# Index scores and attention logits in three rounded products instead of two-pass float32, with the splits on ScalarE and VectorE

## The chip, the cores and the metric

The program runs on one core of a Trainium2 chip. Its engines work side by side and meet through semaphores: PE (TensorE, the matrix products), ACT (ScalarE), DVE (VectorE), POOL (GpSimd) and SP (SyncE, which issues the DMAs). The metric is the device time of one execution in microseconds (us), as the median over runs.

## The reference, cut to what matters

Two layers, each with a feed-forward block, a token mixer, a second feed-forward block and an embedding block, on 256 tokens of 1024 features in float32. The change lies in the token mixer, in the two products below:

```
sc = jnp.einsum('bqhd,bsd->bqhs', qib, ki32)                 # index scores: 8 heads of 64, one key for all heads
I = jnp.einsum('bqh,bqhs->bqs', wib * idx_scale, relu(sc))   # summed over heads; the top 64 keys of a query are kept
...
logits = jnp.einsum('bqhd,bqkhd->bqhk', qb, ksel) * att_scale  # attention logits: 8 heads of 64
prob = softmax(logits masked to the kept keys); out = prob @ v
```

Queries are taken in two blocks of 128. A query of the first block can only see the first 128 keys, one of the second all 256.

## The kernel before, in words

**Weights.** All large products run as chunks: 2048 columns of weights per partition come by DMA into one of three slots of `raw`; ACT rounds them to `w_hi` (float32r, line 903), DVE subtracts to get the rest `w_lo` (line 1303), and PE multiplies in three rounded terms, hi by hi, lo by hi, hi by lo (lines 408 to 410). Such a rounding and rest together are called a split, `split(L, n)`, and stand in the code of ACT and of DVE at fixed places. PE waits for the rest of a slot before it starts the chunk. The chunks of the mixer are numbered from MIX: IQ is MIX+3 and +4 (index queries), GQ +5, GK +6, AQ +7 and +8 (attention queries), AK +9 and +10 (attention keys), GV +11 and +12, GR +13 and +14, and MGA from +15.

**Order.** Nothing is scheduled by a tool: each engine runs its instructions in the order of its function, and PE's order is one long row of chunks with small products between them. Results pass through 8 banks of PSUM; `drained` counts, for each bank, the copies out of it, and `wait_drained` and `wait_free` wait on that count.

**Index scores.** ACT copies the two chunks of index queries from PSUM to `iqT` (line 999). DVE scales the index key into `ikT` (line 1449), and a small DMA (line 361, semaphore `keys_copied`) copies it to the other half of the partitions. After chunk IQ+1 PE runs two transposes (line 571) and then `scores` four times (line 542), each for two heads by two: the heads r = 0 and r = 1 sit in the lower and the upper 64 partitions and write different banks. The operands are plain float32. The trace shows each such matmul as two records of PE and two of its weight loads.

**Attention logits.** ACT copies the queries to `qT` (lines 1028, 1031), DVE scales the keys into `kT` (lines 1498, 1505). `logits(j)` (line 603) multiplies 64 queries at a time, in tiles of 64 by 64 of the array, so four products stand side by side. PE calls `logits(0)` between chunk GV+1 and chunk GR, after four transposes (line 619), once the banks of `aq1` and `ak1` are drained; `logits(2)`, `(4)` and `(6)` come in the loop over MGA, each right behind `levels` (line 690, also 64 by 64). `scores(0)` and `(2)`, `logits(0)` and `(2)` work on 128 keys, the other four calls on 256.

**DVE in this part.** After the scores DVE adds up the heads, picks the top 64 keys of the first query block (`top_k(L, 0)`), makes the decays, picks those of the second block (`top_k(L, 1)`, with `ak0` taken halfway), takes `ak1` and then does splits MIX+13 to MIX+16 in a row. It then waits for the logits.

Of the kernel before, what the change touches and what calls it, by code (L numbers as in the profile page):

```python
# [7 lines left out]
F32 = mybir.dt.float32  # L8
F32R = mybir.dt.float32r
# [4 lines left out]
P = 128  # L14
# [78 lines left out]
def hybrid_trunk(nc, a, out):  # L93
    L_N = a["gla_gate_w2"].shape[0]
    with ExitStack() as ctx:
# [6 lines left out]
        def sem(name):  # L102
            return ctx.enter_context(nc.semaphore(name))
# [37 lines left out]
        pT_hi_, pT_lo_ = (b[:, 2, :].rearrange("p (k t) -> p k t", t=T) for b in (small_hi, small_lo))  # L141
        zg = silu
# [32 lines left out]
        qT = sb("qT", [P, 4, T])  # L175
# [3 lines left out]
        kT = sb("kT", [P, 4, T])  # L179
# [47 lines left out]
        keys_copied = sem("keys_copied")  # L227
        p_landed = sem("p_landed")
# [170 lines left out]
        def _(pe):  # L399
# [123 lines left out]
            def mix(L):  # L523
# [9 lines left out]
                def scores(qT_, kT_, name, j):  # L533

                    qt, _, m = STEPS[j]
                    nk = P * (qt + 1)
                    for r in range(2):
                        wait_free(pe, L, f"{name}{j + r}")
                    for i in range(2):
                        for r in range(2):  # L540
                            rows = slice(64 * r, 64 * r + 64)
                            mm = pe.matmul(bank[BANK_OF[f"{name}{j + r}"]][:, i * nk:(i + 1) * nk], qT_[rows, 2 * m + i, qt * P:(qt + 1) * P],  # L542
                                           kT_(rows, 2 * m + i, nk), start=True, stop=True)
                            if i:
                                done(mm, f"{name}{j + r}")
# [27 lines left out]
                pe.wait_ge(keys_copied, (L + 1) * 16)  # L573
                for j in range(0, 8, 2):
                    if j < 4:
                        wait_drained(pe, L, f"iq{j // 2}")
                    scores(iqT, lambda rows, hp, nk: ikT[rows, 0 if rows.start else 1, 0:nk], "sc", j)
# [14 lines left out]
                def logits(j):  # L592

                    qt, _, m = STEPS[j]
                    nk = P * (qt + 1)
                    for r in range(2):
                        wait_free(pe, L, f"lg{j + r}")
                    for i in range(2):
                        for r in range(2):
                            rows = slice(64 * r, 64 * r + 64)  # L600
                            for c in range(2):
                                at = qt * P + 64 * c
                                mm = pe.matmul(bank[BANK_OF[f"lg{j + r}"]][64 * c:64 * c + 64, i * nk:(i + 1) * nk],  # L603
                                               qT[rows, 2 * m + i, at:at + 64], kT[rows, 2 * m + i, 0:nk], start=True, stop=True)
                            if i:
                                done(mm, f"lg{j + r}")
# [282 lines left out]
        def _(act):  # L889
# [99 lines left out]
            def mix(L):  # L989
# [6 lines left out]
                split(L, MIX + 5)  # L996
                for i in range(2):
# [30 lines left out]
                take(L, "aq0", flat(qT[:, 0:2, :]))  # L1028
                split(L, MIX + 10)
                chunk_products(L, AQ + 1)  # L1030
                take(L, "aq1", flat(qT[:, 2:4, :]))
# [9 lines left out]
                split(L, MIX + 14)  # L1041
                chunk_products(L, GV + 1)
# [247 lines left out]
        def _(dve):  # L1290
# [148 lines left out]
            def mix(L):  # L1439
# [10 lines left out]
                split(L, MIX + 5)  # L1450
                split(L, MIX + 6)
                split(L, MIX + 7)
# [42 lines left out]
                def take_first_keys():  # L1495

                    chunk_products(L, AK)
                    take(L, "ak0", kT[:, 0:2, :])
# [6 lines left out]
                take(L, "ak1", kT[:, 2:4, :])  # L1505
                split(L, MIX + 13)
                split(L, MIX + 14)
                split(L, MIX + 15)
# [369 lines left out]
```

## Time and profile before

| | |
|---|---|
| median of 3 runs | 1175.69 us (1175.69 to 1175.87) |
| profiled execution: its own time | 1175.69 us |
| profiled execution: span from first to last instruction | 1173.9 us |
| mean granted clock of TensorE | 0.998 of full speed |
| PE busy | 1166.0 us, 99% of the span |
| PE weight loads busy | 1142.5 us, 97% |
| DVE, ACT, POOL busy | 820.7, 610.0, 117.3 us |

The time of a run is the span and some 1.8 us around it. A PE share of 99% says that hardly any moment of the span has no matmul record. PE's records overlap (one lasts longer than the step to the next), so the cost of a matmul is read from the distance of starts, not from its own length.

### The profile page before, as it was taken

What the parts mean: (1) busy time and instruction counts of PE and PEld (TensorE: products, weight loads), DVE (VectorE), ACT (ScalarE), POOL (GpSimd) and SP (SyncE); (2) the same over time, 40 slices, a digit from 0 to 9 for tenths busy, and PEclk for the clock granted to TensorE, in tenths of its full rate; (3) what the DMA queues carried; (4) which work ended last, traced back from release to release, by engine and by line L of the source; (5) the groups of instructions that cost most, each with busy time, mean ns of one, the idle gap of its engine ahead of it and who ended that gap; (6) DMA issues with size and microseconds to landing.
All of it is one profiled execution on the core that took longest, in us unless ns stands there. A gap on an engine that the chain in (4) does not pass through costs nothing.

```text
span 1173.9 us, 24028 instructions
## 1 busy us (share of the span) xinstructions
PE 1166.0 (99%) x10518; PEld 1142.5 (97%) x10518; DVE 820.7 (70%) x936; ACT 610.0 (52%) x689; POOL 117.3 (10%) x130
## 2 busy tenths in 40 slices
PE   9999999999999999999999999999999999999998
PEld 9999999999999999999999999999899999999997
DVE  6866545697978766655786665458799787666556
ACT  6544445555745644444764443447466555444455
POOL 2000001011512000001110000100134020000011
PEclk9999999999999999999999999999999999999999
DMA  8655555545445555555546555554644456655551
GB/s 296 230 203 189 190 204 176 188 150 204 152 145 194 202 193 201 191 188 196 192 179 220 184 205 186 184 213 141 218 146 149 140 207 210 203 184 201 190 180 37
DMA packets 33528, 218.87 MB, mean 186 GB/s; under 512 B 5200, under 2 KB 6544, under 8 KB 7440
## 3 DMA queue, kind: packets, MB, share of 16 engines
q1 hardware_dynamic: 33424, 217.34, 53.5%
q8 instruction: 83, 1.36, 0.5%
q14 instruction: 21, 0.17, 0.0%
HBM read 216.15 MB, written 1.05 MB: 185 GB/s over the span
## 4 chain that ended last, share of the span: by engine, by line
PE 98%; DMA 1%; DVE 0%; ACT 0%; SPq 0%; DVEq 0%; issue 0%
PE psum L408 32%; PE psum L409 31%; PE psum L410 31%; PE psum L690 1%; PE psum L669 1%; DMA x_all<-in_x 1%; PE psum L542 0%; PE psum L603 0%; PE psum L653 0%; PE psum L724 0%; DVE gates L1795 0%; PE psum L638 0%; PE psum L735 0%; PE psum L758 0%; DVE hB_lo L1763 0%; PE psum L585 0%
## 5 line engine op out<-in xcount | busy, mean ns | idle before, releaser
L1303 DVE TENSOR_TENSOR w_lo<-raw,w_hi 128x2048 fp32r<-128x2048 f32 x200 | 457.9, 2293 | 218.7 <-ACT w_hi L903 218.5
L903 ACT ACTIVATE w_hi<-raw 128x2048 fp32r<-128x2048 f32 x201 | 385.2, 1916 | 352.2 <-PE psum L410 344.3
L408 PE MATMUL psum<-hA_hi,w_hi 128*128 128x256 f32 x1360 | 377.6, 278 | 0.0
L409 PE MATMUL psum<-hA_hi,w_lo 128*128 128x256 f32 x1360 | 375.7, 276 | 0.0
L410 PE MATMUL psum<-hA_lo,w_hi 128*128 128x256 f32 x1360 | 375.6, 276 | 0.0
L408 PEld LDWEIGHTS psum<-hA_hi,w_hi 128*128 128x128 f32 x1360 | 255.3, 188 | 2.7 <-issue 2.7
L409 PEld LDWEIGHTS psum<-hA_hi,w_lo 128*128 128x128 f32 x1360 | 255.3, 188 | 0.0
L410 PEld LDWEIGHTS psum<-hA_lo,w_hi 128*128 128x128 f32 x1360 | 255.3, 188 | 0.0
L408 PE MATMUL psum<-hB_hi,w_hi 128*128 128x256 f32 x832 | 229.9, 276 | 1.0 <-DVE w_lo L1771 1.0
L409 PE MATMUL psum<-hB_hi,w_lo 128*128 128x256 f32 x832 | 229.7, 276 | 0.0
L410 PE MATMUL psum<-hB_lo,w_hi 128*128 128x256 f32 x832 | 229.7, 276 | 0.0
L410 PE MATMUL psum<-hid_lo,w_hi 128*128 128x256 f32 x704 | 194.3, 276 | 0.0
L408 PE MATMUL psum<-hid_hi,w_hi 128*128 128x256 f32 x704 | 194.3, 276 | 0.0
L409 PE MATMUL psum<-hid_hi,w_lo 128*128 128x256 f32 x704 | 194.3, 276 | 0.0
L408 PEld LDWEIGHTS psum<-hB_hi,w_hi 128*128 128x128 f32 x832 | 156.2, 188 | 1.4 <-DVE w_lo L1771 1.4
L409 PEld LDWEIGHTS psum<-hB_hi,w_lo 128*128 128x128 f32 x832 | 156.2, 188 | 0.0
L410 PEld LDWEIGHTS psum<-hB_lo,w_hi 128*128 128x128 f32 x832 | 156.2, 188 | 0.0
L410 PEld LDWEIGHTS psum<-hid_lo,w_hi 128*128 128x128 f32 x704 | 132.1, 188 | 0.0
L409 PEld LDWEIGHTS psum<-hid_hi,w_lo 128*128 128x128 f32 x704 | 132.1, 188 | 0.0
L408 PEld LDWEIGHTS psum<-hid_hi,w_hi 128*128 128x128 f32 x704 | 132.1, 188 | 0.0
L1223 POOL TENSOR_TENSOR total<-silu 128x256 f32<-128x256 f32 x9 | 9.9, 1102 | 612.9 <-ACT silu L913 612.9
L1382 DVE TENSOR_TENSOR gates<-psum,rb 128x512 f32<-128x512 f32 x44 | 30.3, 690 | 38.7 <-PE psum L410 38.7
(208 smaller groups left out, 1240.7 us busy)
## 6 DMA issues: line engine op xcount, KB each, us to landing
raw<-in_weights SPq DMA_DIRECT2D x203, 1024.0 KB, 4.9
raw<-in_weights SPq DMA_DIRECT2D x2, 512.0 KB, 6.2
out<-gates SPq DMA_DIRECT2D x4, 192.0 KB, 2.2
x_all<-in_x SPq DMA_DIRECT2D x1, 520.0 KB, 3.9
x_all<-in_x SPq DMA_DIRECT2D x1, 512.0 KB, 6.3
relu<-in_p SPq DMA_DIRECT2D x2, 256.0 KB, 5.0
consts<-in_consts SPq DMA_DIRECT2D x1, 384.0 KB, 5.6
out<-gates SPq DMA_DIRECT2D x2, 128.0 KB, 2.0
```

The source lines that it names most:

```text
L408: pe.matmul(o, lh, rh, start=start, stop=False)
L409: pe.matmul(o, ll, rh, start=False, stop=False)
L410: return pe.matmul(o, lh, rl, start=False, stop=stop)
L669: mm = pe.matmul(bank[BANK_OF[f"oa{n}"]][64 * r:64 * r + 64, i * P:(i + 1) * P], v[:, kt, h * 64:(h + 1) * 64], probT[r][:, q * P:(q + 1) ...
L690: mm = pe.matmul(bank[BANK_OF[f"lv{p}{hh}"]][64 * c:64 * c + 64, first + q * cols:first + (q + 1) * cols], kk[rows, q * P + 64 * c:q * P + ...
L903: act.activation(w_hi[:, s, :], raw[:, s, :], ACT.Copy).then_inc(hi_ready[s], 1)
L1223: pool.tensor_tensor(total[:, :], squared[:, 0, :], squared[:, 1, :], ALU.add).then_inc(sq_added, 1)
L1303: dve.tensor_tensor(w_lo[:, s, :], raw[:, s, :], w_hi[:, s, :].bitcast(F32), ALU.subtract).then_inc(lo_ready[s], 1)
L1382: dve.tensor_tensor(up_sum, products(2 * g + 1), both(rb), ALU.mult).then_inc(up_scaled, 1)
```

## The change: three rounded terms, and who makes them

Both products are now made like the weight chunks: operands are split into a rounded part and a rest, and each product is the sum of three float32r matmuls. The logits take 128 queries at a time. The queries are split while they leave PSUM: ACT writes the rounded part, DVE subtracts it from PSUM, and it is DVE's instruction that now frees the bank. The index key is split after its DMA (two copies on ACT, two subtractions on DVE). The attention keys are scaled by DVE as before, into the place of `iqT`, then rounded by ACT and subtracted by DVE. The other parts of the program are as they were. The diff, cut to its core:

```diff
+        iq_hi, iq_lo = oa_hi, oa_lo
+        q_hi, q_lo = obT_hi, obT_lo
+        ik_hi, ik_lo = (b[:, :, :].rearrange("p a t -> p (a t)") for b in (diag_hi, diag_lo))
...
-        qT = sb("qT", [P, 4, T])
+        k_hi = sb("k_hi", [P, 4, T], F32R)
-        kT = sb("kT", [P, 4, T])
+        k_lo = sb("k_lo", [P, 4, T], F32R)
...
PE, scores:
-                    for i in range(2):
-                        for r in range(2):
-                            rows = slice(64 * r, 64 * r + 64)
-                            mm = pe.matmul(bank[...][:, i * nk:(i + 1) * nk], qT_[rows, 2 * m + i, qt * P:(qt + 1) * P],
-                                           kT_(rows, 2 * m + i, nk), start=True, stop=True)
+                        for term, (q, key) in enumerate(((iq_hi, ik_hi), (iq_lo, ik_hi), (iq_hi, ik_lo))):
+                            for r in range(2):
+                                rows = slice(64 * r, 64 * r + 64)
+                                mm = pe.matmul(bank[...][:, i * nk:(i + 1) * nk], q[rows, 2 * m + i, qt * P:(qt + 1) * P],
+                                               key[rows, 0:nk], start=term == 0, stop=term == 2)
-                pe.wait_ge(keys_copied, (L + 1) * 16)
+                pe.wait_ge(ik_lo_ready, (L + 1) * 2)
PE, logits:
-                            for c in range(2):
-                                at = qt * P + 64 * c
-                                mm = pe.matmul(bank[...][64 * c:64 * c + 64, i * nk:(i + 1) * nk],
-                                               qT[rows, 2 * m + i, at:at + 64], kT[rows, 2 * m + i, 0:nk], start=True, stop=True)
+                        for term, (q, key) in enumerate(((q_hi, k_hi), (q_lo, k_hi), (q_hi, k_lo))):
+                            for r in range(2):
+                                mm = pe.matmul(bank[...][:, i * nk:(i + 1) * nk], q[rows, 2 * m + i, qt * P:(qt + 1) * P],
+                                               key[rows, 2 * m + i, 0:nk], start=term == 0, stop=term == 2)
PE, before logits(0):
-                        for name in ("aq1", "ak1"):
-                            wait_drained(pe, L, name)
+                        wait_drained(pe, L, "aq1")
+                        pe.wait_ge(k_lo_ready, (L + 1) * 2)
ACT:
-                    take(L, f"iq{i}", flat(iqT[:, 2 * i:2 * i + 2, :]))
+                    act.activation(flat(iq_hi[:, 2 * i:2 * i + 2, :]), bank[BANK_OF[f"iq{i}"]][:, :], ACT.Copy).then_inc(iq_hi_ready, 1)
                     if i == 0:
                         split(L, MIX + 6)
+                        act.wait_ge(keys_copied, (L + 1) * 16)
+                        for rows, at in copied:
+                            act.activation(ik_hi[rows, :], ikT[rows, at, :], ACT.Copy).then_inc(ik_hi_ready, 1)
...
                 split(L, MIX + 14)
+                for i in range(2):
+                    wait_drained(act, L, f"ak{i}")
+                    act.activation(k_hi[:, 2 * i:2 * i + 2, :], iqT[:, 2 * i:2 * i + 2, :], ACT.Copy).then_inc(k_hi_ready, 1)
                 chunk_products(L, GV + 1)
DVE (rest_of_bank waits for the rounded part, subtracts it from the bank, and counts the bank as drained):
                 split(L, MIX + 6)
+                rest_of_bank(iq_hi_ready, iq_hi, iq_lo, "iq0", 0)
+                for i, (rows, at) in enumerate(((slice(0, 64), 1), (slice(64, 128), 0))):
+                    dve.wait_ge(ik_hi_ready, L * 2 + i + 1)
+                    dve.tensor_tensor(ik_lo[rows, :], ikT[rows, at, :], ik_hi[rows, :].bitcast(F32), ALU.subtract).then_inc(ik_lo_ready, 1)
+                rest_of_bank(iq_hi_ready, iq_hi, iq_lo, "iq1", 1)
                 split(L, MIX + 7)
...
                 distance(64, 63)
+                rest_of_bank(q_hi_ready, q_hi, q_lo, "aq0", 0)
                 split(L, MIX + 11)
+                rest_of_bank(q_hi_ready, q_hi, q_lo, "aq1", 1)
                 top_k(L, 1, halfway=take_first_keys)
...
                 split(L, MIX + 13)
                 split(L, MIX + 14)
+                for i in range(2):
+                    dve.wait_ge(k_hi_ready, L * 2 + i + 1)
+                    dve.tensor_tensor(k_lo[:, 2 * i:2 * i + 2, :], iqT[:, 2 * i:2 * i + 2, :], k_hi[...].bitcast(F32),
+                                      ALU.subtract).then_inc(k_lo_ready, 1)
                 split(L, MIX + 15)
                 split(L, MIX + 16)
```

On PE, the first call of the logits, between the transposes of line 619 (now 628) and chunk GR, stood so:

```order
L619 MATMUL psum<-consts,klev 128x128 x4
L603 MATMUL psum<-kT,qT 64x128 x8
```

and stands now so (`small_hi` and `small_lo` hold the split queries):

```order
L628 MATMUL psum<-consts,klev 128x128 x4
L612 MATMUL psum<-k_hi,small_hi 128x128 x2
L612 MATMUL psum<-k_hi,small_lo 128x128 x2
L612 MATMUL psum<-k_lo,small_hi 128x128 x2
L612 MATMUL psum<-k_hi,small_hi 128x128 x2
L612 MATMUL psum<-k_hi,small_lo 128x128 x2
L612 MATMUL psum<-k_lo,small_hi 128x128 x2
```

Eight products of 64 queries became twelve of 128, with a rest of the keys among their operands.

On DVE, from the second half of `top_k(L, 1)` to the first logits, the order was:

```order
L1437 TENSOR_SCALAR selbias<-score 128x256
L1420 TENSOR_TENSOR kT<-psum,rb 128x512
L1303 TENSOR_TENSOR w_lo<-raw,w_hi 128x2048 x4
L1521 TENSOR_TENSOR relu<-psum,selbias 128x256
```

and is now:

```order
L1453 TENSOR_SCALAR selbias<-score 128x256
L1436 TENSOR_TENSOR iqT<-psum,rb 128x512
L1319 TENSOR_TENSOR w_lo<-raw,w_hi 128x2048 x2
L1540 TENSOR_TENSOR k_lo<-iqT,k_hi 128x512 x2
L1319 TENSOR_TENSOR w_lo<-raw,w_hi 128x2048 x2
L1555 TENSOR_TENSOR relu<-psum,selbias 128x256
```

The subtractions that finish the attention keys stand behind the splits of MIX+13 and MIX+14. Ahead of `top_k(L, 1)` there are two more subtractions:

```order
L1521 TENSOR_TENSOR dist<-bcum 128x512
L1471 TENSOR_TENSOR small_lo<-psum,small_hi 128x512
L1319 TENSOR_TENSOR w_lo<-raw,w_hi 128x2048
L1471 TENSOR_TENSOR small_lo<-psum,small_hi 128x512
L1445 MEMSET score 64x64
```

where before the `dist` instruction, one `w_lo` and the MEMSET followed each other.

On DVE ahead of the scores, the three splits of MIX+5 to MIX+7 that stood in a row now have the rests of the index queries and of the key between the second and the third:

```order
L1319 TENSOR_TENSOR w_lo<-raw,w_hi 128x2048 x2
L1471 TENSOR_TENSOR small_lo<-psum,small_hi 128x512
L1478 TENSOR_TENSOR diag_lo<-ikT,diag_hi 64x256 x2
L1471 TENSOR_TENSOR small_lo<-psum,small_hi 128x512
L1319 TENSOR_TENSOR w_lo<-raw,w_hi 128x2048
L1491 TENSOR_SCALAR score<-relu,wi 128x128
```

## Rows read from the trace of the kernel before

**Rows 1.** The page: chain of work that ended last, by engine.

```profile
PE 98%; DMA 1%; DVE 0%; ACT 0%; SPq 0%; DVEq 0%; issue 0%
```

**Rows 2.** Waits of PE, the longest: us in total, times, longest.

```profile
PE psum L855 <- POOL ones_r L1235: 1.2, 1, 1.2
```

**Rows 3.** Chain of work in time: start us, us; a 256-key call.

```profile
295.11 0.89 PE psum L603 x16
```

**Rows 4.** Timeline, PE weight loads: start us, us, line, shape.

```profile
214.43 2.58 PEld L542 LDWEIGHTS psum<-ikT,iqT 64*128 64x128 f32 x32 [0.17 <-issue]
...
217.34 0.19 PEld L408 LDWEIGHTS psum<-hA_hi,w_hi 128*128 128x128 f32 x1 [0.33 <-issue]
217.45 0.19 PEld L409 LDWEIGHTS psum<-hA_hi,w_lo 128*128 128x128 f32 x1
...
262.62 0.42 PEld L603 LDWEIGHTS psum<-kT,qT 64*64 64x64 f32 x16 [0.17 <-issue]
263.22 0.19 PEld L408 LDWEIGHTS psum<-w_hi,hA_hi 128*128 128x128 f32 x1 [0.17 <-issue]
```

**Rows 5.** The same view: calls 2 and 4 of the logits, levels to attend.

```profile
281.63 0.43 PEld L603 LDWEIGHTS psum<-kT,qT 64*64 64x64 f32 x16
282.23 0.20 PEld L653 LDWEIGHTS psum<-consts,prob 128*128 128x128 f32 x2 [0.17 <-issue]
...
294.43 0.56 PEld L690 LDWEIGHTS psum<-amat,silu 64*64 64x64 f32 x32
294.90 0.65 PEld L603 LDWEIGHTS psum<-kT,qT 64*64 64x64 f32 x16
295.93 0.13 PEld L669 LDWEIGHTS psum<-probT,v 128*64 128x64 f32 x1 [0.39 <-issue]
...
323.57 0.33 PEld L690 LDWEIGHTS psum<-amat,silu 64*64 64x64 f32 x16
323.94 0.13 PEld L669 LDWEIGHTS psum<-probT,v 128*64 128x64 f32 x1
```

**Rows 6.** Weight loads of 128 columns by form: end sums of one column, transposes.

```profile
1165.82 0.41 PEld L871 LDWEIGHTS psum<-ones_r,total 128*128 128x128 f32 x3
...
L653 PEld LDWEIGHTS psum<-consts,prob 128*128 128x128 f32 x48 | 5.4, 139 | 0.3 <-issue 0.3
```

**Rows 7.** Timeline, ACT and DVE, ahead of the scores.

```profile
214.32 0.60 ACT L984 ACTIVATE iqT<-psum 128x512 f32<-128x512 f32 x1 [3.04 <-PE psum L410]
...
211.32 2.29 DVE L1303 TENSOR_TENSOR w_lo<-raw,w_hi 128x2048 fp32r<-128x2048 f32 x1 [3.13 <-ACT w_hi L903]
216.82 2.29 DVE L1303 TENSOR_TENSOR w_lo<-raw,w_hi 128x2048 fp32r<-128x2048 f32 x1 [3.22 <-ACT w_hi L903]
```

**Rows 8.** Timeline, DVE, from the last keys on.

```profile
259.20 0.68 DVE L1420 TENSOR_TENSOR kT<-psum,rb 128x512 f32<-128x512 f32 x1
259.80 4.48 DVE L1303 TENSOR_TENSOR w_lo<-raw,w_hi 128x2048 fp32r<-128x2048 f32 x2
265.39 2.29 DVE L1303 TENSOR_TENSOR w_lo<-raw,w_hi 128x2048 fp32r<-128x2048 f32 x1 [1.11 <-ACT w_hi L903]
```

**Rows 9.** The same place in layer 1: PE loads and DVE.

```profile
840.67 0.43 PEld L603 LDWEIGHTS psum<-kT,qT 64*64 64x64 f32 x16 [0.17 <-issue]
...
837.80 4.48 DVE L1303 TENSOR_TENSOR w_lo<-raw,w_hi 128x2048 fp32r<-128x2048 f32 x2
```

**Rows 10.** Durations (ns min/median/max) of a subtraction or product in SBUF.

```profile
L1385 DVE TENSOR_TENSOR gates<-gates x44: 691/692/694, 30.4 to 1078.7; 128x512 f32<-128x512 f32 x44
L1356 DVE TENSOR_TENSOR diag_lo<-total,diag_hi x6: 410/418/420, 24.6 to 1144.1; 128x256 fp32r<-128x256 f32 x6
```

**Rows 11.** Clock: warm-up matmuls; windows at the end (busy, PEclk third from last).

```profile
1.21 6.03 PE L855 MATMUL psum<-ones_r 128*128 128x128 f32 x36 [1.21 <-POOL ones_r L1235]
...
1166.40:1168.80 2.40, 1.83 (x12) 1.40 (x11) 1.62 (x8) 1.89 (x6) 0.00 (x0) 1.00 0.00 0
1168.80:1170.00 1.20, 0.00 (x0) 0.00 (x0) 1.20 (x4) 0.00 (x0) 0.00 (x0) 0.53 0.18 63
```

More of the change, by code:

```diff
@@ L227, in hybrid_trunk @@
         keys_copied = sem("keys_copied")
+        ik_hi_ready = sem("ik_hi_ready")
+        ik_lo_ready = sem("ik_lo_ready")
+        iq_hi_ready = sem("iq_hi_ready")
+        q_hi_ready = sem("q_hi_ready")
+        k_hi_ready = sem("k_hi_ready")
+        k_lo_ready = sem("k_lo_ready")
         p_landed = sem("p_landed")
@@ L531, in chunk, with scores @@
                     return s
-                def scores(qT_, kT_, name, j):
+                def scores(j):
                     qt, _, m = STEPS[j]
@@ L537, in scores @@
                     for r in range(2):
-                        wait_free(pe, L, f"{name}{j + r}")
+                        wait_free(pe, L, f"sc{j + r}")
                     for i in range(2):
-                        for r in range(2):
-                            rows = slice(64 * r, 64 * r + 64)
-                            mm = pe.matmul(bank[BANK_OF[f"{name}{j + r}"]][:, i * nk:(i + 1) * nk], qT_[rows, 2 * m + i, qt * P:(qt + 1) * P],
-                                           kT_(rows, 2 * m + i, nk), start=True, stop=True)
-                            if i:
-                                done(mm, f"{name}{j + r}")
+                        for term, (q, key) in enumerate(((iq_hi, ik_hi), (iq_lo, ik_hi), (iq_hi, ik_lo))):
+                            for r in range(2):
+                                rows = slice(64 * r, 64 * r + 64)
+                                mm = pe.matmul(bank[BANK_OF[f"sc{j + r}"]][:, i * nk:(i + 1) * nk], q[rows, 2 * m + i, qt * P:(qt + 1) * P],
+                                               key[rows, 0:nk], start=term == 0, stop=term == 2)
+                                if i and term == 2:
+                                    done(mm, f"sc{j + r}")
                 for t in range(2):
@@ L576, in mix @@
                         wait_drained(pe, L, f"iq{j // 2}")
-                    scores(iqT, lambda rows, hp, nk: ikT[rows, 0 if rows.start else 1, 0:nk], "sc", j)
+                    scores(j)
                 chunk(GQ, "gq")
@@ L598, in logits @@
                     for i in range(2):
-                        for r in range(2):
-                            rows = slice(64 * r, 64 * r + 64)
-                            for c in range(2):
-                                at = qt * P + 64 * c
-                                mm = pe.matmul(bank[BANK_OF[f"lg{j + r}"]][64 * c:64 * c + 64, i * nk:(i + 1) * nk],
-                                               qT[rows, 2 * m + i, at:at + 64], kT[rows, 2 * m + i, 0:nk], start=True, stop=True)
-                            if i:
-                                done(mm, f"lg{j + r}")
+                        for term, (q, key) in enumerate(((q_hi, k_hi), (q_lo, k_hi), (q_hi, k_lo))):
+                            for r in range(2):
+                                rows = slice(64 * r, 64 * r + 64)
+                                mm = pe.matmul(bank[BANK_OF[f"lg{j + r}"]][:, i * nk:(i + 1) * nk], q[rows, 2 * m + i, qt * P:(qt + 1) * P],
+                                               key[rows, 2 * m + i, 0:nk], start=term == 0, stop=term == 2)
+                                if i and term == 2:
+                                    done(mm, f"lg{j + r}")
                 for n, c in [(GV, "gv"), (GR, "gr")]:
@@ L1027, in mix @@
                 chunk_products(L, AQ)
-                take(L, "aq0", flat(qT[:, 0:2, :]))
+                act.activation(flat(q_hi[:, 0:2, :]), bank[BANK_OF["aq0"]][:, :], ACT.Copy).then_inc(q_hi_ready, 1)
                 split(L, MIX + 10)
                 chunk_products(L, AQ + 1)
-                take(L, "aq1", flat(qT[:, 2:4, :]))
+                act.activation(flat(q_hi[:, 2:4, :]), bank[BANK_OF["aq1"]][:, :], ACT.Copy).then_inc(q_hi_ready, 1)
                 split(L, MIX + 11)
```

10 lines of the change are left out of this document (8 added, 2 removed).

## The prediction

> **What bounds the kernel now.** I read the page first: the chain of work that ended last is PE for 98% of the span [rows 1]. The view of waits is the second: PE waits at three places, all at the start or the end of the span, and the longest wait is 1.2 us [rows 2]. So between these PE runs without a break. Each microsecond that the change adds to PE's row of loads and matmuls, or in which PE finds an operand unfinished, is a microsecond of the whole, since PE has no later wait in which it could be made up. The other engines count only where they make PE wait. So there are three questions: what the new products cost PE, when the split operands are ready, and when PE would want them. The third view is the timeline of PE's weight loads, whose starts are exact; the fourth is the timeline of ACT and DVE at the same places. Times below are those of layer 0.
>
> **PE: the unit prices.** A plain float32 matmul is two passes. With 256 keys a call of the logits takes 0.89 us for four steps (two values of i, two passes; the tiles beside each other share a step), 0.22 us a step [rows 3]. With 128 keys the whole call takes, from its first load to the next chunk's, 0.60 us [rows 4], and a step is some 0.11 us. A rounded term is one pass: the loads of chunks with 256 columns are 0.11 us apart [rows 4]. A rounded term with only 128 columns is nowhere in the trace. Upper bound: the same 0.11 to 0.12. Lower bound: the transposes, whose two loads are 0.20 - 0.14 = 0.06 us apart [rows 5, 6]. I take 0.11, since the load itself sets it: at the end three loads of 128 columns, each with a matmul of one column, take 0.41 us, that is (0.41 - 0.19) / 2 = 0.11 us a step though almost nothing is streamed [rows 6], and the loads of rounded chunks last 0.19 us like these, not 0.14 us like the transposes' [rows 4, 6]. So three terms cost 0.34 us. That is 0.10 us less than two passes with 256 keys (0.44) and 0.12 us more than two passes with 128 (0.22). There are as many steps of one kind as of the other, so in bare products the change gives PE next to nothing.
>
> On this the Trainium skill, TensorE: Matmul & The Clock Gate, section Back-to-back issue gap, gives about 56 ns for a warm matmul of 128 columns counted by itself. By it the 24 terms a layer with 128 columns would be 0.055 us cheaper each, 1.3 us a layer. Its section on LDWEIGHTS gives 107 ns for a load of 128 columns, and with that the row at the end of the trace agrees.
>
> **PE: the scores.** The key's rest must be ready. DVE ends split MIX+6 at 211.32 + 2.29 = 213.61 [rows 7]. Behind it come the rest of iq0 (0.69 us as other work on 512 elements [rows 10]; the next instruction starts 0.08 before its end) to 214.2, and two rests of the key at 0.42 [rows 10] less the same overlap, to 214.83. ACT has rounded the key by 211.9 (two short copies behind its split, whose end at 211.3 is what DVE's split waits for [rows 7]), so DVE is last. With 0.05 us for the semaphore PE starts at 214.90 instead of 214.43 [rows 4]: a wait of 0.47. The first call takes 6 steps, 0.67 us, to 215.57. The second needs the rest of iq1: ACT ends its rounding at 214.92 [rows 7], DVE's subtraction follows to 215.66, so the call starts at 215.72. Then 17 steps of 0.114 to the last load at 217.66. The way out: behind a 256-key call of the logits the next load is 295.93 - (294.90 + 0.65 - 0.13) = 0.51 us after the last load of the call, behind a 128-key call 263.22 - (262.62 + 0.42 - 0.13) = 0.31 us [rows 4, 5], in both cases two of the call's last steps and 0.09. A rounded 256-column term has a step of 0.11, so 0.31. Chunk GQ then loads at 217.98 instead of 217.34 [rows 4]: **+0.64 us**.
>
> **DVE: how late the attention keys are.** From 219 us on DVE has no idle time until the pair of splits ends at 264.3; I read the timeline row by row, and its end stands in [rows 8]. The subtractions inserted ahead of the scores end at 215.7, in the 3.22 us in which DVE waited for ACT [rows 7], so they cost DVE nothing. The two rests of the attention queries are different: they stand where DVE is full, and add 2 times 0.61 = 1.22 us to all that follows. The take of ak1 moves from 259.20 to 260.42 and the pair of splits from 259.80 to 261.02 [rows 8]. The next instruction can start 4.40 us later, so the rests of the keys start at 265.42. ACT has rounded the keys long before: ak1 is drained at 261.1, plus some 0.6. Two subtractions of 128x512 in SBUF, 0.61 and 0.69 us [rows 10], end at **266.71**.
>
> **PE: the first logits.** PE would load for them at 262.62 + 0.64 = 263.26 [rows 4]. Before, it only needed the take of ak1, done at 259.88 [rows 8]. Now it needs the rests, at 266.71 + 0.05. **The wait is 3.50 us.** Behind PE's waiting load stands all the rest of the layer. No weight chunk adds to it: MIX+13, the first half of the pair, ends at 262.1 + 1.22 = 263.3 and is wanted at 263.22 + 0.64 = 263.86 even without the wait [rows 4, 8], and behind the pair DVE had 1.11 us of idle time [rows 8]. The call itself: 5 steps of 0.112 and a way out of 0.27 (between 0.20 and 0.31) are 0.83 against 0.60 us: **+0.23**.
>
> **PE: the other calls.** Before, the logits' loads followed those of `levels` at once (294.90 against a last load at 294.43 + 0.56 - 0.13 = 294.86), since both use 64 by 64 tiles [rows 5]. Now the tile is 64 by 128. From `levels` to the attend products, another change of form, the step is 323.94 - (323.57 + 0.33 - 0.13) = 0.17 us [rows 5]. Call 2: 0.17 + 0.56 + 0.27 = 1.00 against 0.04 + 0.60 = 0.64 us (281.63 to 282.23) [rows 5]: **+0.36**. Calls 4 and 6: 0.17 + 0.57 + 0.31 = 1.05 against 1.07 us (294.86 to 295.93) [rows 5]: **0**.
>
> **The sum.** 0.64 + 3.50 + 0.23 + 0.36 = 4.73 us a layer. Layer 1 has the same distances: PE's load for the first logits starts 2.87 us behind DVE's pair of splits, in layer 0 it is 2.82 us [rows 4, 8, 9]. Twice 4.73 is 9.5 us. The profiled execution's own time is 1175.69 us and so is the median, so I predict **1185.2 us**, 0.8% slower.
>
> **The rivals.**
>
> *The clock falls in the wait.* At the end of the trace PE has 12 matmul records in 2.40 us, still at a granted clock of 1.00; in the next 1.2 us, with none, the mean is 0.53 [rows 11], so it went from 2.4 to 1.2 GHz behind a thin stretch. In the forecast PE does nothing for 3.50 us, twice. The price of coming back is bounded by the warm-up: 36 loads in 6.03 us [rows 11], where 36 steps of 0.11 would be 4.0, so 2.0 us. With one fall 1187.2, with two 1189.2. Against it: in the chunks before and behind the wait PE is dense, which it was not at the end of the trace. The same page of the Trainium skill, section HAM oscillation, says that a PE which idles between bursts of matmuls is put back to half clock and pays for it each time; by that rule both layers pay. I give 22% to one or both.
>
> *The two heads do not run beside each other when rounded.* The plain float32 tiles of 64 rows do. The trace has no rounded matmul on 64 rows. If each pair cost two steps, the 24 pairs of the scores and the 24 of the logits a layer are 2.7 us each. But PE would then want the keys 2.7 us later and wait 0.8 instead of 3.5: 0.64 + 2.7 + 0.8 + 0.23 + 0.36 + 2.7 = 7.4 us a layer, 1190.6. 7%, since loads of both kinds have the same duration.
>
> *The keys are in time, the other side.* If DVE ended the rests of the keys when PE wants them, 3.5 us earlier than in my count, 1.23 us a layer stay: 1178.2. If the 128-column terms also ran at the 0.06 us of the transposes, 24 of them would save 1.2 us a layer and the time would be 1175.7, no slower than before. It decides at 263.2 us, the end of `k_lo`. For it speaks only that the order of DVE could be shortened by something that I count as full; against it, the pair of splits alone ends at 264.3 before anything is added [rows 8]. 8%, of which 3 for slower. (The cheap terms alone, with the wait, give about 1184: PE comes earlier and waits longer, so only what lies behind the wait is gained.)
>
> *The forecast*: 63%, 1183.5 to 1186.5.
>
> **How the numbers follow.** A measurement of this kernel tells about 0.2% (2.4 us) from no change. Faster by more takes the last rival and something yet unseen, 2%; within 0.2% 3%; the rest is slower, 95%. For the range I leave out the keys in time and the serial heads, and reach from the forecast with its cheap bounds (128-column terms at 0.06, the wait some tenths shorter: 1183.0) to the clock falling in both layers (1189.2).
>
> **What the profile after would show.** PE's waits should have a new row at the logits' line for DVE's `k_lo`, two times 3.5 us, and one at the scores' line for DVE's rests, about 0.5 us a layer. DVE's busy time grows by some 9 us. The loads of the rounded terms on 64 rows should come in pairs, 0.11 us from pair to pair for 128 and for 256 keys. The granted clock stays near 0.998; a fall right behind the wait is the first rival. The prediction is wrong if `k_lo` does not end 3.5 us, give or take 0.5, behind PE's arrival, or if the pairs are 0.06 or 0.22 us apart.

## The result and the profile after

The changed kernel takes **1190.84 us** (median of 4 runs, 1190.43 to 1191.04), the kernel before 1175.70 beside it: a ratio of 1.0128, 95% interval 1.0115 to 1.0140, 15.1 us slower. The forecast was 1185.2 with a range to 1189.2, so the sign is right, the size is too small by 5.6 us, and the time lies outside the range.

The view of cores of the changed kernel (span, mean granted clock of TensorE; before it was 1173.9 us and 0.998), then its page, parts 1 and 4:

```profile
core 0: 1189.2 us, clock 0.993
```

```profile
PE 1173.0 (99%) x10518; PEld 1150.4 (97%) x10518; DVE 829.4 (70%) x952; ACT 614.1 (52%) x697; POOL 117.2 (10%) x130
...
PE 97%; DVE 1%; issue 1%; DMA 1%; ACT 0%; SPq 0%; DVEq 0%
```

The chain is still PE [rows 1], but it has two gaps ("issue", 1%). PE's waits, to compare with [rows 2] (us in total, times, longest):

```profile
PE psum L612 <- issue: 7.6, 2, 3.8
PE psum L864 <- POOL ones_r L1251: 1.2, 1, 1.2
PE psum L552 <- DVE diag_lo L1478: 1.1, 2, 0.5
```

L612 is the logits' product, L552 the scores'. The view names "issue" for the wait of 3.8 us, not DVE; the timelines show whom it is for. DVE and PE's loads around the first logits call of layer 0, for [rows 8] and [rows 4] (the first two rows of DVE are from further ahead; the part on the prediction comes back to them):

```profile
217.06 2.29 DVE L1319 TENSOR_TENSOR w_lo<-raw,w_hi 128x2048 fp32r<-128x2048 f32 x1 [1.26 <-ACT w_hi L912]
...
232.63 0.30 DVE L1450 MAX8 top<-score 128x8 f32<-128x128 f32 x1 [0.52 <-DVE score L1452]
...
260.96 0.68 DVE L1436 TENSOR_TENSOR iqT<-psum,rb 128x512 f32<-128x512 f32 x1
261.56 4.48 DVE L1319 TENSOR_TENSOR w_lo<-raw,w_hi 128x2048 fp32r<-128x2048 f32 x2
265.96 1.28 DVE L1540 TENSOR_TENSOR k_lo<-iqT,k_hi 128x512 fp32r<-128x512 f32 x2
```

```profile
267.32 0.21 PEld L612 LDWEIGHTS psum<-k_hi,small_hi 64*128 64x128 f32 x2 [4.05 <-issue]
267.42 0.22 PEld L612 LDWEIGHTS psum<-k_hi,small_lo 64*128 64x128 f32 x2
...
267.87 0.22 PEld L612 LDWEIGHTS psum<-k_lo,small_hi 64*128 64x128 f32 x2
268.16 0.19 PEld L417 LDWEIGHTS psum<-w_hi,hA_hi 128*128 128x128 f32 x1
268.27 0.19 PEld L418 LDWEIGHTS psum<-w_hi,hA_lo 128*128 128x128 f32 x1
268.56 0.33 PEld L419 LDWEIGHTS psum<-w_lo,hA_hi 128*128 128x128 f32 x1
268.99 0.33 PEld L417 LDWEIGHTS psum<-w_hi,hA_hi 128*128 128x128 f32 x1
```

The rests of the keys end at 265.96 + 1.28 = 267.24, PE's first load starts at 267.32. The loads of the call come in pairs ("x2": both heads), 0.11 us from pair to pair. Then comes what the forecast did not have: from 268.56 on a load lasts 0.33 us instead of 0.19, and the loads are 0.43 us apart where the same loads of this chunk were 0.23 apart in the kernel before:

```profile
263.33 0.19 PEld L409 LDWEIGHTS psum<-w_hi,hA_lo 128*128 128x128 f32 x1
263.56 0.19 PEld L410 LDWEIGHTS psum<-w_lo,hA_hi 128*128 128x128 f32 x1
```

The windows (start and end, length, then the busy time of PE, its weight loads, DVE, ACT and POOL) show the granted clock, third from last, in the wait and behind it, and then behind the same wait in layer 1:

```profile
263.50:267.00 3.50, 0.01 (x1) 0.00 (x0) 3.50 (x4) 3.16 (x4) 0.00 (x0) 1.00 0.62 169
267.00:269.00 2.00, 1.65 (x15) 1.41 (x16) 2.00 (x2) 0.00 (x0) 0.00 (x0) 0.86 1.08 430
269.00:271.00 2.00, 2.00 (x6) 1.61 (x5) 0.45 (x1) 0.00 (x0) 0.00 (x0) 0.50 0.93 315
271.00:273.00 2.00, 2.00 (x8) 1.60 (x8) 0.00 (x0) 0.00 (x0) 0.00 (x0) 0.79 0.92 385
273.00:275.00 2.00, 2.00 (x10) 1.62 (x10) 0.00 (x0) 0.00 (x0) 0.00 (x0) 1.00 0.36 147
```

```profile
851.00:853.00 2.00, 0.84 (x8) 0.88 (x10) 2.00 (x3) 0.51 (x2) 0.00 (x0) 0.78 1.04 434
853.00:855.00 2.00, 2.00 (x11) 1.67 (x10) 1.26 (x1) 0.00 (x0) 0.00 (x0) 0.50 0.99 410
855.00:857.00 2.00, 2.00 (x6) 1.54 (x5) 0.00 (x0) 0.00 (x0) 0.00 (x0) 0.50 0.93 307
857.00:859.00 2.00, 2.00 (x6) 1.52 (x6) 0.00 (x0) 0.00 (x0) 0.00 (x0) 0.52 0.73 307
859.00:861.00 2.00, 2.00 (x10) 1.62 (x9) 0.00 (x0) 0.00 (x0) 0.00 (x0) 1.00 0.01 4
```

0.50 is 1.2 GHz of 2.4. In layer 0 the clock is still full in the wait itself, and PE had been at work again for over 1 us (from 267.32 to the load at 268.56) when it fell. The time lost is about the missing clock times the window: in layer 0 2 x (0.14 + 0.50 + 0.21) = 1.7 us, in layer 1 2 x (0.22 + 0.50 + 0.50 + 0.48) = 3.4 us.

**Where the 15.1 us are.** PE executes the same loads of weight chunks in the same order in both kernels. The start of each, less the start of the same load before, gives a shift; what it gains between two stations is the cost of what lies between. This table, worked out from the traces, holds those gains in us, layer 0 / layer 1, for the changed kernel and the experiments; everything not listed gains under 0.1 us, but for 0.47 us in e10, told there:

```
                        scores       first call   call 2       whole trace
                                     (to MGA0)
changed kernel          0.73 / 0.70  5.69 / 7.19  0.39 / 0.39  15.1
e1 late call            0.73 / 0.73  0.74 / 0.70  0.83 / 0.82   4.6
e2 rests between        0.70 / 0.70  1.94 / 1.90  0.39 / 0.39   6.0
e3 dummies in the wait  0.70 / 0.70  4.13 / 4.09  0.39 / 0.39  10.4
e4 logits only          0.01 / 0.01  7.51 / 5.91  0.39 / 0.39  14.2
e6 wait alone           0.00 / 0.00  6.66 / 5.81  0.00 / 0.00  12.5
e7 late, query early    0.63 / 0.63  0.84 / 0.75  0.82 / 0.85   4.5
e8 late, all orders     0.63 / 0.63  1.01 / 1.00  0.77 / 0.80   4.9
e9 before, late call    0.01 / 0.01 -0.35/ -0.35  0.98 / 1.01   1.3
e10 rests on GpSimd     0.69 / 0.71  1.17 / 3.47  0.39 / 0.39   7.4
```

For the changed kernel: scores 1.4, call 2 0.8, first calls 12.9. e3 has the same waits and, as told there, no fall of the clock: its first calls gain 4.13 and 4.09, which is 0.23 for the rounded call, as forecast, and 3.9 for the wait (the view of waits, which goes by matmuls, has 3.8). What the changed kernel has above that, 1.56 and 3.10, together 4.7 us, is the fall. It is a little less than the 5.1 us of missing clock, since at full clock these loads are 0.23 us apart and not half of 0.43.

### The profile page after: what moved, and what is told of

Same layout as the page of the kernel before. It is cut to its first block, busy times and chain, and to the rows that moved or that the text cites. A ratio compares the mean times of both kernels' runs of the same rounds, so it can differ in the third digit from the quotient of the medians.

```text
span 1189.2 us, 24052 instructions
## 1 busy us (share of the span) xinstructions
PE 1173.0 (99%) x10518; PEld 1150.4 (97%) x10518; DVE 829.4 (70%) x952; ACT 614.1 (52%) x697; POOL 117.2 (10%) x130
## 4 chain that ended last, share of the span: by engine, by line
PE 97%; DVE 1%; issue 1%; DMA 1%; ACT 0%; SPq 0%; DVEq 0%
PE psum L417 31%; PE psum L418 31%; PE psum L419 31%; PE psum L612 1%; PE psum L699 1%; PE psum L678 1%; DMA x_all<-in_x 1%; PE psum L552 1%; PE psum L662 0%; DVE w_lo L1319 0%; ACT w_hi L912 0%; PE psum L733 0%; DVE gates L1829 0%; PE psum L744 0%; PE psum L647 0%
## 5 line engine op out<-in xcount | busy, mean ns | idle before, releaser
L417 PE MATMUL psum<-hA_hi,w_hi 128*128 128x256 f32 x1360 | 377.6, 278 | 0.0
L417 PEld LDWEIGHTS psum<-hA_hi,w_hi 128*128 128x128 f32 x1360 | 255.4, 188 | 2.3 <-issue 2.0
L417 PE MATMUL psum<-hB_hi,w_hi 128*128 128x256 f32 x832 | 229.9, 276 | 0.7 <-DVE w_lo L1805 0.7
L417 PE MATMUL psum<-hid_hi,w_hi 128*128 128x256 f32 x704 | 194.3, 276 | 0.0
L417 PEld LDWEIGHTS psum<-hB_hi,w_hi 128*128 128x128 f32 x832 | 156.2, 188 | 1.1 <-DVE w_lo L1805 1.1
L417 PEld LDWEIGHTS psum<-hid_hi,w_hi 128*128 128x128 f32 x704 | 132.2, 188 | 0.0
```

Source lines behind the costliest of these rows:

```text
L417: pe.matmul(o, lh, rh, start=start, stop=False)
```

## The experiments

The experiments are numbered e1 to e10. Each time below is a median; the kernel before, run beside it on the same chip, took 1175.75 to 1175.83 us, and the ratio to it stands behind with its 95% interval. "Theory" is from e1 on: the wait costs its length, and the fall of the clock behind it some 5 us more.

**e1, the first logits call late** (behind the output-gate chunk GR):

```
                         done(mm, "kdT")
-                        wait_drained(pe, L, "aq1")
-                        pe.wait_ge(k_lo_ready, (L + 1) * 2)
-                        logits(0)
...
+                wait_drained(pe, L, "aq1")
+                pe.wait_ge(k_lo_ready, (L + 1) * 2)
+                logits(0)
                 wait_drained(pe, L, "kdT")
```

> The changed kernel, with the first call of the logits moved on PE from before chunk GR to behind it, some 11 us later; DVE and ACT keep their order. My theory (the wait for the rests of the keys and the clock that falls in it are 12.5 to 13 us of the 15.1, the products themselves the rest): the keys are ready long before PE wants them, no wait, clock near 0.998, and what stays is 0.72 us a layer at the scores, 0.38 at the second call and some 0.25 at the first, so 1178.4 us. Rival A (rounded products on 64 rows bring the clock down by themselves, wherever they stand): the clock stays near 0.993 and the time is near 1183. Rival B (the logits' mask on DVE and the exponentials behind it now come too late for the gates' chunks): a new PE wait behind MGA, more than 1180.

1180.29 us, 1.0038 [1.0023, 1.0053], clock 0.998. The wait and the fall are gone together, with 10.5 of the 15.1 us. It is 1.9 us above what was expected; its waits show two that were not there before, for a split of DVE (L417) and for the recurrent state (L662). Rival B, a new wait of PE and more than 1180, came in this form:

```profile
PE psum L552 <- DVE diag_lo L1478: 1.1, 2, 0.5
PE psum L417 <- DVE w_lo L1319: 0.9, 2, 0.5
PE psum L662 <- DVE state L1595: 0.8, 2, 0.4
```

**e2, the wait shorter**: the rests of the keys between the two splits, not behind them.

```
                 split(L, MIX + 13)
-                split(L, MIX + 14)
                 for i in range(2):
                     dve.wait_ge(k_hi_ready, L * 2 + i + 1)
                     dve.tensor_tensor(k_lo[:, 2 * i:2 * i + 2, :], iqT[:, 2 * i:2 * i + 2, :], k_hi[:, 2 * i:2 * i + 2, :].bitcast(F32),
                                       ALU.subtract).then_inc(k_lo_ready, 1)
+                split(L, MIX + 14)
```

> The changed kernel, with DVE's two subtractions for the keys moved ahead of split MIX+14 (behind MIX+13 as before), one split of 2.2 us earlier. My theory: PE's wait at the first logits falls from 3.8 to 1.6 us a layer, 4.4 us less in both; a wait of 1.6 us leaves the clock up, which gives 5.1 back: 1190.8 - 9.5 = 1181.3 us. If the clock falls even in the shorter wait: 1186.4. If the wait was not set by DVE's order but by ACT's roundings or the take of the keys, nothing moves: 1190.8.

1181.79 us (1181.65 to 1183.31), 1.0055 [1.0038, 1.0072].

```profile
PE psum L612 <- issue: 3.2, 2, 1.6
```

With 1.6 us of wait the clock stayed: window 267 to 269 us has 1.00. The fourth run, at 1183.31, is 1.5 us above the median with a mean clock of 0.997 where the other three have 0.998 and 0.999; e10 comes back to it.

**e3, the wait filled**: as the changed kernel, but PE works while it waits.

```
+                        wait_free(pe, L, "lg0")
+                        for _ in range(17):
+                            pe.matmul(bank[BANK_OF["lg0"]][:, 0:P], ones[:, :], ones[:, :], start=True, stop=True)
                         wait_drained(pe, L, "aq1")
```

> The changed kernel, with 17 matmuls of 128 by 128 that nobody reads (34 passes, some 3.8 us) in front of the wait for the keys, into the bank that the first logits overwrite. It leaves out nothing. PE is busy in the time in which it waited. My theory (the clock falls because PE does nothing there, and costs 5.1 us over both layers, 1.7 and 3.4): the wait stays as lost time, the clock stays up, 1185.7 us, give or take 0.5 for the length of the filling. Rival (the fall has another cause, as the rounded products): clock 0.993 again and 1190.8 us or more.

1186.07 us, 1.0088 [1.0072, 1.0103], clock 0.998. Timeline of PE (matmuls):

```profile
263.19 3.96 PE L632 MATMUL psum<-ones_r 128*128 128x128 f32 x34
267.20 0.33 PE L612 MATMUL psum<-k_hi,small_hi 64*128 64x128 f32 x2
```

From the last transpose before it to the first load of the call 4.19 us pass in layer 0, in both kernels, so the time for which nothing useful is done is the same, and still 4.8 us are gone: PE's idleness costs them, beyond its own length. The change plus products that nobody reads is faster than the change.

**e4, the logits only** (the scores, their queries and their key as before, none of the rests for them on DVE and ACT):

```
-                        for term, (q, key) in enumerate(((iq_hi, ik_hi), (iq_lo, ik_hi), (iq_hi, ik_lo))):
...
+                        for r in range(2):
+                            rows = slice(64 * r, 64 * r + 64)
+                            mm = pe.matmul(bank[BANK_OF[f"{name}{j + r}"]][:, i * nk:(i + 1) * nk], qT_[rows, 2 * m + i, qt * P:(qt + 1) * P],
+                                           kT_(rows, 2 * m + i, nk), start=True, stop=True)
...
-                rest_of_bank(iq_hi_ready, iq_hi, iq_lo, "iq0", 0)
```

> Only the logits in three rounded terms; the index scores stay in plain float32, the key's DMA is waited for by PE as before. My theory: PE arrives 0.72 us earlier a layer at the first logits while DVE is hardly earlier, so the wait grows to 4.3 us and the scores' cost turns into wait: 1175.7 + 2 x (4.3 + 0.25 + 0.38) + 5.1 for the clock = 1190.7 us, the same as the full change. Rival (the costs of the two parts add): 1190.8 - 1.4 = 1189.4 us.

1189.52 us, 1.0117 [1.0102, 1.0132], nearer the rival than the theory: the waits are 4.1 us at most, 0.3 longer than in the changed kernel, since DVE comes earlier too (its rests of the keys end at 266.86, not 267.24). The profiled execution is the slowest of its four, 1190.09. Here layer 0 has the long fall and layer 1 the short one (7.51 / 5.91 in the table; the changed kernel has 5.69 / 7.19).

**e5, the scores only** (the mirror of e4: the logits, their queries and keys as before).

> The index scores in three rounded terms, the attention logits in float32 as before. In the changed kernel the loads of the chunk behind the scores started 0.72 us (layer 0) and 0.71 us (layer 1) later, 0.5 us of it the wait for the key's rest. Theory (the two halves add up): 1175.8 + 1.4 = 1177.2 us, clock as before, no wait at the first logits call. Rival (the scores' later vector work is what costs at the logits too): the vector engine's 1.7 us of rests come back as a wait at the attention's own keys, 1178.5 us or more.

1177.16 us, 1.0011 [1.0002, 1.0021], as expected to 0.1 us. Its profiled execution took 6214.8 us, for a reason that nothing here shows, and no row of it is read; that PE does not wait at the first logits follows from the time alone. The two halves add up: e4's 13.7 and e5's 1.4 us are the change's 15.1.

**e6, the wait alone.** The kernel before, all products in float32:

```
+                        pe.wait_ge(keys_held, (L + 1) * 4)
                         logits(0)
...
                 split(L, MIX + 14)
...
+                for i in range(4):
+                    if i > 1:
+                        dve.wait_ge(keys_held, L * 4 + i - 1)
+                    k = kT[:, i % 2 * 2:i % 2 * 2 + 2, :]
+                    dve.tensor_tensor(iqT[:, i % 2 * 2:i % 2 * 2 + 2, :], k, k, ALU.subtract).then_inc(keys_held, 1)
```

> The kernel before, with all its float32 products, but the first logits call of each layer waits for four small vector operations (their results are not used) behind the pair of splits, so that TensorE stands for about 3.8 us there. Theory (the idle time by itself makes the clock fall, and half clock costs what it cost in the changed kernel): 1175.8 + 2 x 3.8 + 5 = 1188.4 us, with 3.4 to 6.8 us of half clock behind each wait. Rival (it takes the rounded products' short bursts as well): 1175.8 + 7.6 = 1183.4 us, clock 1.00 behind the waits.

1188.16 us, 1.0104 [1.0091, 1.0118], clock 0.994. Its wait and three windows:

```profile
PE psum L604 <- issue: 8.4, 2, 4.2
```

```profile
265.00:267.50 2.50, 0.62 (x12) 0.65 (x16) 2.50 (x4) 0.82 (x2) 0.00 (x0) 0.55 1.01 413
267.50:269.50 2.00, 2.00 (x16) 1.38 (x9) 1.37 (x1) 0.00 (x0) 0.00 (x0) 0.50 0.63 250
269.50:271.50 2.00, 2.00 (x6) 1.54 (x5) 0.00 (x0) 0.00 (x0) 0.00 (x0) 0.50 0.82 209
```

There is no rounded logits product in it and the clock falls alike, in layer 0 already within the wait (0.55 in the first window, in most of which PE stands). So of the 12.5 us by which its span is longer 8.4 are waits, and 4.1 the fall. The part of a fall that lies in the wait costs nothing, since PE does nothing there that could be slowed: in layer 0 6.66 - 4.2 = 2.5 us are lost, though the clock was at half for 6.8 us.

**e7 and e8, the late call with better orders.** e7 moves one line, DVE's rest of iq0, from behind `split(L, MIX + 6)` to ahead of it; e8 is e7 with the loop of the keys' rests moved from ahead of `split(L, MIX + 15)` to behind `split(L, MIX + 16)`.

> The changed kernel with the first logits call behind the output-gate chunk (as in the run with the late call, 1180.3 us), and the vector engine takes the rest of the first index queries ahead of the split of weights 6 instead of behind it (it idles 3 us there). The wait of 0.5 us ahead of the scores should be gone in both layers: 1180.3 - 1.0 = 1179.3 us. Rival (the split then ends later and the chunk behind the scores waits for it): 1180.3 us.

> As the run with the query's rest early, and the two rests of the attention's keys stand behind the splits 15 and 16 instead of ahead of them. The wait of 0.5 us for a split's low half (two, in the run with the late call) should go too: 1179.3 - 0.9 = 1178.4 us, of which what is left over the kernel before is 0.2 us of scores, 0.4 us of call 2 and 0.4 us of a wait for the recurrent state in each layer, 0.2 us of the first call. Rival (the keys' rests come too late for the late call): a wait of 1 us or more at the first logits call, 1180 us or more.

1180.18 us (1.0037 [1.0023, 1.0051]) and 1180.70 (1.0041 [1.0028, 1.0053]): both missed. In e7 the wait at the scores is only 0.1 us shorter, and for another operand, and the split's wait stays:

```profile
PE psum L417 <- DVE w_lo L1319: 1.1, 2, 0.6
PE psum L662 <- DVE state L1595: 0.8, 2, 0.4
PE psum L552 <- DVE small_lo L1471: 0.7, 2, 0.4
```

What waits now is the second scores call, for iq1's rest (ACT rounds that bank at 214.42, DVE subtracts at 215.11 in the changed kernel). The prediction had this step, "so the call starts at 215.72" (215.86 in the trace), and the expectation of e7 left it out. And e8 refutes my reading of e1's second wait: it is not the keys' rests that make the split late. (Its own rival named the right time for a wrong reason: the new wait at the first logits call is 0.2 us, not 1.) In e1 DVE stood idle ahead of it, for ACT:

```profile
271.72 2.29 DVE L1319 TENSOR_TENSOR w_lo<-raw,w_hi 128x2048 fp32r<-128x2048 f32 x1 [2.36 <-ACT w_hi L912]
```

**e9, what the late place itself costs**: e1's move in the kernel before, float32 throughout.

> The kernel before with nothing changed but the place of the first logits call, behind the output-gate chunk as in the late-call run of the changed kernel (1180.3 us, 4.5 us above before, of which the index scores are 1.4 us). It tells what of the other 3.1 us is the price of the late place itself. Theory (the late place makes the softmax of the first heads late, so the waits of 0.4 us for the recurrent state and 0.5 us for a split's low half in each layer come with it whatever the products are): 1175.8 + 2 x 0.9 = 1177.6 us. Rival (the place is free and the rounded products and keys' rests cost all of it): 1175.8 us.

1177.06 us, 1.0010 [1.0001, 1.0019]; the wait for the state is there, twice as long, the one for the split is not:

```profile
PE psum L653 <- DVE state L1561: 1.9, 2, 0.9
```

So of e1's 4.5 us 1.4 are the scores, 1.3 the place, and 1.8 (0.9 a layer) the rounded products and what they bring: 0.23 and 0.39 of the two calls, and 0.3 that I have not placed.

**e10, the rests off DVE**, the call in its place of before. ACT copies the attention queries in float32 too (`take`, for aq0 and aq1), GpSimd subtracts (`query_rest`):

```
+                take(L, "aq0", flat(q_raw[:, 0:2, :]))
...
+                    pool.tensor_tensor(q_lo[:, 2 * i:2 * i + 2, :], q_raw[:, 2 * i:2 * i + 2, :],
+                                       q_hi[:, 2 * i:2 * i + 2, :].bitcast(F32), ALU.subtract).then_inc(q_lo_ready, 1)
+
+                query_rest(0)
...
                 pool.tensor_tensor(klev[:, :], gkT[:, :], lev[:, :], ALU.mult).then_inc(lev_ready, 1)
+                query_rest(1)
                 pool.tensor_tensor(qdec[:, :], gqT[:, :], qdec[:, :], ALU.mult).then_inc(lev_ready, 1)
...
+                pool.tensor_tensor(k_lo[:, 0:2, :], iqT[:, 0:2, :], k_hi[:, 0:2, :].bitcast(F32), ALU.subtract).then_inc(k_lo_ready, 1)
...
-                rest_of_bank(q_hi_ready, q_hi, q_lo, "aq0", 0)
...
                 split(L, MIX + 13)
...
+                dve.tensor_tensor(k_lo[:, 2:4, :], iqT[:, 2:4, :], k_hi[:, 2:4, :].bitcast(F32), ALU.subtract).then_inc(k_lo_ready, 1)
                 split(L, MIX + 14)
```

> The changed kernel, first logits call at its place of before, with the rests taken off the full vector engine: ScalarE also copies the attention queries in float32 to a buffer that is free there, GpSimd subtracts both query rests and the first keys' rest, and the vector engine takes the second keys' rest between splits 13 and 14. By the timelines the take of the last keys then ends at 260.2, split 13 at 262.4, the second rest at 263.1 us, and TensorE comes at 263.4: no wait, so no fall of the clock. Theory (the rest of the changed kernel's cost is the steps on TensorE: scores 0.72, first call 0.23, call 2 0.38 a layer): 1175.8 + 2.7 = 1178.5 us. Rival (the copies and rests on the other engines make something else late, as GpSimd's first level product or the splits on ScalarE): 1180 us or more, with a new wait of TensorE.

1183.01 us (1.0055 [1.0042, 1.0069]), and the runs fall in two groups, 1181.31 and 1181.43 against 1183.01, 1183.01 and 1183.34. The rival came, in a form that I had not named. Timelines of GpSimd and DVE:

```profile
237.70 1.30 POOL L1267 TENSOR_TENSOR small_lo<-prob,small_hi 128x512 fp32r<-128x512 f32 x1 [41.92 <-ACT prob L995]
...
260.51 1.39 POOL L1278 TENSOR_TENSOR k_lo<-iqT,k_hi 128x512 fp32r<-128x512 f32 x1 [8.85 <-ACT k_hi L1061]
```

```profile
237.87 3.27 DVE L1334 TENSOR_TENSOR w_lo<-raw,w_hi 128x2048 fp32r<-128x2048 f32 x1
...
261.26 2.78 DVE L1334 TENSOR_TENSOR w_lo<-raw,w_hi 128x2048 fp32r<-128x2048 f32 x1
263.97 0.68 DVE L1552 TENSOR_TENSOR k_lo<-iqT,k_hi 128x512 fp32r<-128x512 f32 x1
```

In layer 0 the splits that meet a subtraction of GpSimd take 3.27 and 2.78 us, not 2.28: 0.99 and 0.50 more, about as long as the two lie together (237.87 to 239.00 and 261.26 to 261.90). The first makes PE wait 0.47 us for its weights, and DVE takes the last keys at 260.66 where the changed kernel had 260.96: of the 1.2 us taken off DVE 0.3 were gained. The Trainium skill, SBUF — State Buffer, section SBUF: two separate sides, says that DVE (with two SBUF inputs) and GpSimd share a port pair which one holds for a whole instruction; the trace agrees. In layer 1 it shows the other order: here the split begins first and keeps its length, GpSimd's subtraction takes 3.24 us instead of 1.30, and the next instruction of DVE pays, 1.78 us where it took 0.68 before:

```profile
818.55 3.24 POOL L1267 TENSOR_TENSOR small_lo<-prob,small_hi 128x512 fp32r<-128x512 f32 x1 [41.95 <-DVE gkT L1451]
```

```profile
818.35 2.28 DVE L1334 TENSOR_TENSOR w_lo<-raw,w_hi 128x2048 fp32r<-128x2048 f32 x1
820.55 1.78 DVE L1526 SCALAR_TENSOR_TENSOR dist<-silu,hidden 128x512 f32<-128x512 f32 x1
```

PE still waits at the logits' call, up to 1.6 us:

```profile
PE psum L614 <- issue: 2.5, 2, 1.6
```

And behind the wait of 1.6 us, in layer 1, the clock fell this time. The call's first load is at 845.79, the clock is full until 847, and then (windows 847 to 849, mean 0.61, and 849 to 851):

```profile
849.00:851.00 2.00, 2.00 (x6) 1.51 (x6) 1.13 (x1) 0.00 (x0) 0.00 (x0) 0.53 1.01 356
```

By the table that layer's first call costs 2.3 us more than layer 0's, 0.7 of it the longer wait and 1.6 the fall, which is also the 1.6 us between the medians of the two groups of runs; the three longer ones have mean clocks of 0.996 and 0.997, the two others 0.998 and 0.999. e2's fourth run is 1.5 us off, which would fit one fall; no profile shows that run, nor one of e10's two shorter runs. Why the clock falls behind one wait of 1.6 us and not behind another is therefore open, and only the waits of 3.8 us and more made it fall in both layers of every profile.

## Why the prediction was wrong

- **The clock, the step that failed.** "The clock falls in the wait" was a rival at 22%. It happened in both layers: gone without the wait (e1), gone with the wait filled (e3), there with the wait alone (e6). It took 4.7 of the 5.6 us that the forecast was short. (In the changed kernel's layer 0 the clock fell behind the wait, not in it.) My argument against it, "in the chunks before and behind the wait PE is dense, which it was not at the end of the trace", is refuted by e6: PE is as dense around that wait. The row for it lay in [rows 11], where the mean was down to 0.53 in the 1.2 us behind the last matmul; a wait three times as long as that should have been given the larger chance. With the two-falls time of 1189.2 as the forecast, 1.6 us would have been missing.
- **The price of a fall** was "bounded by the warm-up", 2.0 us, and that was no bound: the warm-up shows one recovery, and a fall lasted about 3.4 us (price 1.6) or 6.8 us (price 3.1, or 2.5 where its start lay in the wait). In the changed kernel they are together 5.1 us by the windows, 4.8 by the times of e3 and the changed kernel, 4.7 by their traces, where two times 2.0 had been allowed. The Trainium skill, TensorE: Matmul & The Clock Gate, section HAM oscillation, which I had weighed for the chance alone, also prices the fall: the extra time is half of the throttled time. For the two stretches here, 10.2 us, that is an estimate of 5.1 us; the traces have 4.7.
- **The wait** was 3.9 us by loads (3.8 by the view of waits), forecast 3.50. The rests ended at 267.24, forecast 266.71; PE came 0.1 later too. DVE's chain was 0.54 us later than counted: the pair of splits starts at 261.56, not 261.02. Two things stood at nothing in the sum. The subtractions ahead of the scores "cost DVE nothing", but the split behind them starts at 217.06, not 216.82 [rows 7], since ACT's rounding for it starts at 215.11, not 214.88; some 0.1 us of this is in all starts of that trace before it. And a pause in `top_k(L, 0)` is 0.52 us (the MAX8 at 232.63), where the kernel before had 0.21. All seven traces with rounded scores have it, at 0.51 or 0.52, the four with float32 scores have 0.18 to 0.21; what makes it, no run shows. Size off, mechanism right.
- **The scores** cost 0.73 and 0.70, forecast 0.64, with the wait of 0.5 at the key's rest, the second call after it, and 0.11 us between pairs. The sum for the end of the key's rests was 0.07 short in its own terms (214.90, not 214.83), and in the trace they do not overlap and end at 214.22 + 0.86 = 215.08.
- **Call 2** 0.39, forecast 0.36; **the first call** 0.24 (from its first load to the next chunk's 268.16 - 267.32 = 0.84, against 0.60 in [rows 4]), forecast 0.23; **calls 4 and 6** under 0.1, forecast 0.
- **The unit price** of a rounded term with 128 columns, bounded by 0.06 and 0.11, is 0.11: 267.32, 267.42 ... 267.87 are five steps in 0.55. The lower bound does not hold here, where each matmul has a load of its own. The 56 ns of the Trainium skill, TensorE: Matmul & The Clock Gate, section Back-to-back issue gap, are for a matmul without that, as the section says; they were no bound for this step.
- **The heads beside each other**: yes, since the loads come in twos within a step of 0.11. That rival (7%) is out; that its 1190.6 us is close to the measured time is chance.
- **The keys in time** (8%): e1, with the wait gone but the call late, gives 1180.29; e10 did not bring them in time. The 1178.2 us of that rival were therefore not reached by any kernel here, and stay a sum.

In numbers, the 5.6 us by which the forecast was short: fall of the clock 4.7, the two waits 0.8, scores and call 2 0.2 (each rounded).

No version here beats the kernel before. The best with both products rounded, e7, is 4.4 us slower; the scores alone (e5) cost 1.4.

## What to carry to other kernels

A wait of TensorE on a path where it is the bound can cost more than its length (here 7.8 us of waits cost 12.4): in windows behind it, read the granted clock, and price the missing clock times the window. Before adding an operand that a full engine has to finish, count on that engine what stands ahead of it; two subtractions of 0.6 us and a place behind two splits made 3.8 us of wait here. If the wait can't be removed, shorten it (e2), or fill it (e3), or let TensorE do something else first (e1). Work moved from VectorE to GpSimd can still hold up VectorE where both read SBUF (e10).

## What the runs showed of the hardware that was not expected

- Idle time of 3.8 to 4.2 us of TensorE, between dense stretches, brought it to half clock each of the six times in the profiles of the changed kernel, e4 and e6; the half-clock stretch was 3.4 or 6.8 us, with the same kernel in either layer.
- A wait of 1.6 us did it in one place (e10, layer 1) and not in another (e2, both layers), and the times of e10's runs, in two groups, fit a fall in some runs and none in others.
- Seventeen idle float32 products in each wait, 4.0 us long, kept the clock at 0.998 and made the kernel 4.8 us faster.
- A DVE split of 2.28 us took up to 3.27 beside a GpSimd subtraction of 1.3 us that had begun first; where the split had begun first, the subtraction took 3.24 (e10).
